# Gate and up of the last FFN as 2x2 blocks with seven products instead of eight

## What is computed

```python
D_FF_2 = ((8 * D_MODEL // 3 + 255) // 256) * 256      # 2816
h2 = rmsnorm_2(x, norm2_g[l])
g = jnp.einsum('bsd,df->bsf', h2, w_gate[l])
u = jnp.einsum('bsd,df->bsf', h2, w_up[l])
x = x + jnp.einsum('bsf,fd->bsd', jax.nn.silu(g) * u, w_down[l])
return rmsnorm_2(x, normf_g)
```

## Time and profile before

| | |
|---|---|
| time, median of 3 runs | 1824.26 us (1824.08 to 1824.57) |
| profiled execution: its span from first to last instruction | 1822.8 us |
| difference of the median to that span | 1.5 us |
| TensorE busy, mean granted clock | 1810.1 us (99%), 0.998 |
| VectorE, ScalarE, GpSimd busy | 938.6, 727.8, 272.3 us |
| last FFN, first gate matmul to last down matmul | 1451.3 to 1810.3 us |

### The profile page before, as it was taken

One profiled execution on the slowest core, in us unless ns is written; L12 is line 12 of the kernel. 1 busy time (PEld: TensorE's weight loads), 2 busy tenths in 40 slices (PEclk: granted clock), 3 DMA queues, 4 the chain that ended last, 5 costly groups with the idle time before them and its releaser, 6 DMA issues.

```text
span 1822.8 us, 21331 instructions
## 1 busy us (share of the span) xinstructions
PE 1810.1 (99%) x8733; PEld 1472.7 (81%) x8733; DVE 938.6 (51%) x1429; ACT 727.8 (40%) x1155; POOL 272.3 (15%) x241
## 2 busy tenths in 40 slices
PE   9999999999999999999999999999999999999998
PEld 7877788888888887878888888877777888888886
DVE  6878556443453456545653345458667443333324
ACT  5644444331332435654432233332567432212223
POOL 2001222210121200002221022103001222101210
PEclk9999999999999999999999999999999999999999
DMA  6121123222222333212223222232121132222221
GB/s 243 67 88 66 70 95 114 93 93 94 91 95 96 118 128 108 82 47 93 93 95 113 93 93 95 91 110 99 70 103 59 70 109 100 93 92 93 102 89 64
DMA packets 32337, 173.41 MB, mean 95 GB/s; under 512 B 4064, under 2 KB 6240, under 8 KB 14320
## 3 DMA queue, kind: packets, MB, share of 16 engines
q1 hardware_dynamic: 26848, 162.55, 25.0%
q10 hardware_dynamic: 5392, 9.51, 1.6%
HBM read 169.38 MB, written 2.13 MB: 94 GB/s over the span
## 4 chain that ended last, share of the span: by engine, by line
PE 96%; ACT 1%; DVE 1%; DMA 0%; POOL 0%; issue 0%; SPq 0%; ACTq 0%; DVEq 0%; POOLq 0%
PE ps L995 54%; PE ps L1299 20%; PE ps L929 7%; PE ps L1014 5%; PE ps L1141 2%; PE ps L1186 2%; PE ps L1166 2%; PE ps L1034 1%; PE ps L1225 1%; PE ps L1206 1%; DMA raw<-in_wall 0%; ACT PC L1543 0%; DVE WL L1806 0%; ACT WH L1375 0%; POOL sq L2326 0%
## 5 line engine op out<-in xcount | busy, mean ns | idle before, releaser
L995 PE MATMUL ps<-hH,WH 128*128 128x512 f32 x1456 | 570.9, 392 | 0.1
L1806 DVE TENSOR_TENSOR WL<-raw,WH 128x1024 fp32r<-128x1024 f32 (+2 forms) x308 | 377.3, 1264 | 368.1 <-ACT WH L1375 367.9
L995 PE MATMUL ps<-hH,WL 128*128 128x512 f32 x1456 | 566.7, 389 | 0.0
L995 PE MATMUL ps<-hL,WH 128*128 128x512 f32 x1456 | 566.7, 389 | 0.0
L1375 ACT ACTIVATE WH<-raw 128x1024 fp32r<-128x1024 f32 (+2 forms) x308 | 301.4, 1026 | 311.8 <-PE ps L1299 228.6
L995 PEld LDWEIGHTS ps<-hH,WH 128*128 128x128 f32 x1456 | 273.3, 188 | 65.3 <-issue 7.3
L995 PEld LDWEIGHTS ps<-hH,WL 128*128 128x128 f32 x1456 | 273.3, 188 | 57.0
L995 PEld LDWEIGHTS ps<-hL,WH 128*128 128x128 f32 x1456 | 273.3, 188 | 56.9 <-issue 1.0
L1299 PE MATMUL ps<-fL,WH 128*128 128x512 f32 x531 | 205.9, 388 | 0.0
L1299 PE MATMUL ps<-fH,WL 128*128 128x512 f32 x531 | 205.9, 388 | 0.0
L1299 PE MATMUL ps<-fH,WH 128*128 128x512 f32 x531 | 205.9, 388 | 0.0
(11 more groups left out here) (369 smaller groups left out, 2020.7 us busy)
## 6 DMA issues: line engine op xcount, KB each, us to landing
raw<-in_wall SPq DMA_DIRECT2D x140, 1024.0 KB, 4.6
raw<-in_wall SPq DMA_DIRECT2D x12, 768.0 KB, 4.0
bias<-in_bias ACTq DMA_DIRECT2D x12, 256.0 KB, 3.3
X<-in_xt SPq DMA_DIRECT2D x8, 256.0 KB, 8.9
CB<-rows ACTq DMA_DIRECT2D x8, 256.0 KB, 3.3
raw<-in_wall SPq DMA_DIRECT2D x4, 256.0 KB, 5.8
mrA<-in_memt ACTq DMA_DIRECT2D x4, 256.0 KB, 6.3
Mb<-m_rows ACTq DMA_DIRECT2D x4, 256.0 KB, 4.8
```

The lines of the kernel that those rows point to most:

```text
L995: mm = e.matmul(ps[b][:, 0:N], ww[:, k, c:c + 128], x[:, k, 0:N], start=(k == 0 and i == 0), stop=(k == 7 and i == 2))
L1806: e.tensor_tensor(WL[n % NCV][:, c], raw[n % NRAW][:, c], WH[n % NCV][:, c].bitcast(F32), ALU.subtract).then_inc(*mark("wl", n, x))
```

## The change

Only the last FFN changes (`WINO = (2,)`). Its first pair of units (block s = 0) is computed as before, in four tiles of 512 columns (steps `wg0`, `wu0`). For each of the ten later pairs, s = 1 to 10, the gate and up weights are cut in a 2x2 of blocks (even and odd k-tiles; gate and up) and the tokens in two halves of 256, and seven products (Strassen's, in Winograd's form) take the place of eight. Each product (`wp`) has K = 512 and 256 gate or up features: 4 k-tiles x 2 tiles x 3 parts = 24 matmuls of 256 columns. They run in the order q1, q5, q6, q3, q7, q2, q4. q1, q6, q7 and q4 add up in one PSUM bank; so q6 waits until ScalarE has copied the bank after q1 (`wcopy`), q7 until it has copied it after q6, q4 after q7. q5 and q3 share a second bank, q2 has a third.

Products 5, 6, 3 and 7 take sums of weight blocks, made on VectorE (`wsum`, 1024 columns each) ahead of their conversion; products 5, 6, 4 and 7 take sums of activation halves. Those are made by `wt`, once for each pair p = 0 to 3 of X tiles: a scaled copy of 256 columns on ScalarE, four scalar_tensor_tensor of 256 columns on VectorE (T5, T7, T6, T4), a rounding of 768 columns on ScalarE (TH), a subtraction of 768 columns on VectorE (TL). `wt` 0 and 1 stand behind the `res_norm` of tiles 5 and 6, `wt` 2 and 3 behind the two gate tiles of block 0. `wt7` overwrites part of hH and hL once block 0 is through.

Weights are converted in chunks of 1024 columns (`cconv`), four places of WH/WL in turn, so the conversion for product n+3 stands ahead of product n in the list and waits for product n-1. A block has seven chunks to convert where it had four. There are three raw buffers; per block two gate/up units and one down unit are loaded. `down` moves into the stream: after the products of a block come one or two pieces `wd` (24 matmuls of 512 columns each, one piece for s = 1 and 2, two from s = 3), and VectorE adds each output tile to X (`wx`; with the tail 48 additions where there were 16); the last 4 k-tiles stay as a tail. The number of down matmuls does not change. Per block VectorE also adds c12 and c11 from PSUM, multiplies by R (1024 columns), makes c22, z1 and z0; ScalarE copies four banks and does SiLU and H in 1024 columns, GpSimd y and L in 1024 columns each.

The core of the diff:

```diff
+WINO = (2,)
+PRODUCTS = (1, 5, 6, 3, 7, 2, 4)
...
+def wino_sequence():
+
+    out = []
+    for s in range(1, NSU):
+        out += [("q", s, q) for q in PRODUCTS] + [("d",) + x for x in down_pieces(s)]
+    return out
+
+
...
+            two(("U1", s), block(gate, g, 0), block(up, u, 0))
+            if x[2] != 1:
+                two(("U2", s), block(up, u, 1), block(gate, g, 1))
...
+                at = block_of(q)
+                if at:
+                    c["unit"], c["at"] = ROLE[i, at[0], s], at[1] * CHUNK
+                else:
+                    c["sum"] = {5: ((units[0], CHUNK), (units[1], 0)), 6: ((i, "q", s, 5), (units[0], 0)),
+                                3: ((i, "q", s, 6), (units[1], CHUNK)), 7: ((units[0], 0), (units[0], CHUNK))}[q]
+                    c["place"] = {5: 0, 6: 1, 3: 0, 7: 1}[q]
...
+                if nrm in WINO_OF and m in (5, 6):
+                    put("wt", WINO_OF[nrm], m - 5)
...
+    def ffn_wino(i, end):
+        late = []
+
+        def used(key):
+            done.add(("chunk", CHUNK_AT[key]))
+
+        for p, _ in enumerate(g_fm(1, FFN_NORMS[i], f"g{i}", "wg0")):
+            put("wt", i, 2 + p)
+        for _ in g_fm(1, FFN_NORMS[i], f"u{i}", "wu0"):
+            conv_ahead(len(UNITS))
+        flush_norms()
+        put("wt7", i)
+        for x in SEQUENCE:
+            conv_ahead(len(UNITS))
+            if x[0] == "d":
+                _, g, c = x
+                put("wd", i, g, c)
+                while late:
+                    put(*late.pop(0))
+                used((i, "d", g, c))
+                put("wx", i, g, c)
+                continue
+            _, s, q = x
+            put("wp", i, s, q)
+            while late:
+                put(*late.pop(0))
+            used((i, "q", s, q))
+            if q in (1, 5, 6, 7):
+                put("wcopy", i, s, q)
+            elif q == 3:
+                put("wc12", i, s)
+            elif q == 2:
+                put("wc11", i, s)
+                put("wgate", i, s)
+            else:
+                put("wz1", i, s)
+                late.append(("wz0", i, s))
+        while late:
+            put(*late.pop(0))
+        hread = ("wq", i, NSU - 1, 4)
+        if i == 2:
+            put("sqrt_table")
+        for mg in (0, 1):
+            n = ROLE[i, "T", mg]
+            now["unit"] = n + 1
+            conv_ahead(n + 2)
+            for gi, ks in TAIL[mg]:
+                for mi in range(4):
+                    put("wtail", i, mg, gi, mi, n, ks)
+                    if gi == 2:
+                        put("res_ffn", i, 1, 4 * mg + mi, hread)
+            done.add(n)
+        if end:
+            rstd(end, 60)
+
     def ffn(i, acts, end):
+        if i in WINO:
+            ffn_wino(i, end)
...
+                elif what == "wp":
+
+                    i, st, pn = a
+                    c = CHUNK_AT[i, "q", st, pn]
+                    kind = {1: "wA", 6: "wA", 7: "wA", 4: "wA", 5: "wD", 3: "wD", 2: "wB"}[pn]
+                    opens = pn in (1, 5, 2)
+                    if opens:
+                        b, before = bank((kind, i, st), {"wA": ("wg", "z", 0), "wD": ("wg", "c12"), "wB": ("wg", "c11")}[kind] + (i, st),
+                                         hold=kind == "wA")
+                        if before:
+                            w.wait_ge(*at(*before))
+                    b = BANK[kind, i, st]
+                    if not opens:
+                        w.wait_ge(*at("wcopy", i, st, {6: 1, 7: 6, 4: 7, 3: 5}[pn]))
+                    w.wait_ge(*at("wl", "c", c))
+                    W = [x.rearrange("p (k c) -> p k c", k=4) for x in chunk_slot(c)]
+                    for p in range(4):
+                        w.wait_ge(*at(*moving_at(i, pn, p)))
+                        H, L = moving(pn, p)
+                        for u in (0, 1):
+                            for n, (ww, x) in enumerate(((W[0], H), (W[0], L), (W[1], H))):
+                                mm = e.matmul(ps[b][:, 256 * u:256 * u + 256], ww[:, p, 128 * u:128 * u + 128], x,
+                                              start=(opens and p == 0 and u == 0 and n == 0),
+                                              stop=(p == 3 and u == 1 and n == 2), skip_group_check=True)
+                    mm.then_inc(*mark("wq", i, st, pn))
+                    FREED["chunk", c] = ("wq", i, st, pn)
...
+                elif what == "cconv":
+                    c = a[0]
+                    if CHUNKS[c]["sum"]:
+                        w.wait_ge(*at("wg", "sum", c))
+                    else:
+                        w.wait_ge(*loaded(CHUNKS[c]["unit"]))
+                    for b in W_BEFORE["chunk", c]:
+                        w.wait_ge(*at(*FREED[b]))
+                    e.activation(chunk_slot(c)[0], chunk_src(c), ACT.Copy).then_inc(*mark("wh", "c", c))
...
+                elif what == "wt":
+                    i, p = a
+                    st = FFN_NORMS[i]
+                    if p:
+                        w.wait_ge(*at("wg", "t", "L", i, p - 1))
+                    w.wait_ge(*at("xo", OUT_OF[i], 2 * p))
+                    e.activation(Tf[:, 3, :], X[:, 2 * p, 256:512], ACT.Copy, scale=col(st, 2 * p)).then_inc(
+                        *mark("wcopy", "t", "B", i, p))
+                    w.wait_ge(*at("wg", "t", 4, i, p))
+                    e.activation(TH[:, p, :, :], Tf[:, 0:3, :], ACT.Copy).then_inc(*mark("wcopy", "t", "H", i, p))
+
...
+                elif what == "wcopy":
+                    i, st, pn = a
+                    dst = {1: held_q1, 5: held_q5, 6: held_v, 7: held_w}[pn]
+                    w.wait_ge(*at("wq", i, st, pn))
+                    if st == 1:
+                        w.wait_ge(*(at("wg", "t", "L7", i) if pn in (6, 7) else at("wg", "t", "L", i, 3)))
+                    else:
+                        w.wait_ge(*at(*{1: ("wg", "c11"), 5: ("wg", "z", "c22"), 6: ("wg", "c12"), 7: ("wg", "z", 1)}[pn], i, st - 1))
+                    e.activation(dst[:, :, :], by_tile(BANK["wD" if pn == 5 else "wA", i, st]), ACT.Copy).then_inc(
+                        *mark("wcopy", i, st, pn))
+
...
+                    w.wait_ge(*at("wg", "ng", i))
+                    w.wait_ge(*at("wcopy", "t", "B", i, p))
+                    e.scalar_tensor_tensor(out=Tf[:, 0, :], in0=a0, scalar=g[:, 2 * p:2 * p + 1], in1=Tf[:, 3, :],
+                                           op0=ALU.mult, op1=ALU.subtract).then_inc(*mark("wg", "t", 5, i, p))
+                    w.wait_ge(*at("xo", OUT_OF[i], 2 * p + 1))
+                    e.scalar_tensor_tensor(out=T7f[:, p, :], in0=a3, scalar=g[:, 2 * p + 1:2 * p + 2],
+                                           in1=Tf[:, 3, :], op0=ALU.mult, op1=ALU.subtract).then_inc(
+                        *mark("wg", "t", 7, i, p))
+                    w.wait_ge(*at("wg", "t", 5, i, p))
+                    e.scalar_tensor_tensor(out=Tf[:, 1, :], in0=a3, scalar=ng[:, 2 * p + 1:2 * p + 2],
+                                           in1=Tf[:, 0, :], op0=ALU.mult, op1=ALU.subtract).then_inc(
+                        *mark("wg", "t", 6, i, p))
+                    w.wait_ge(*at("wg", "t", 6, i, p))
+                    e.scalar_tensor_tensor(out=Tf[:, 2, :], in0=a1, scalar=ng[:, 2 * p + 1:2 * p + 2],
+                                           in1=Tf[:, 1, :], op0=ALU.mult, op1=ALU.subtract).then_inc(
+                        *mark("wg", "t", 4, i, p))
+                    w.wait_ge(*at("wcopy", "t", "H", i, p))
+                    e.tensor_tensor(TL[:, p, :, :], Tf[:, 0:3, :], TH[:, p, :, :].bitcast(F32),
+                                    ALU.subtract).then_inc(*mark("wg", "t", "L", i, p))
+
+                elif what == "wt7":
+                    i = a[0]
+                    w.wait_ge(*at("wcopy", "t", "H7", i))
+                    e.tensor_tensor(hL[:, 0:8:2, 256:512], T7f[:, :, :], hH[:, 0:8:2, 256:512].bitcast(F32),
...
+                        w.wait_ge(*at("wsilu", i, st - 1))
+                    e.tensor_tensor(gs[:, :, 256:512], by_tile(BANK["wD", i, st]), held_v[:, :, :], ALU.add).then_inc(
+                        *mark("wg", "c12", i, st))
...
+                    R = Rsb[:, :].rearrange("p (o t) -> p o t", o=1).broadcast_to([128, 2, 512])
+                    e.tensor_tensor(gs[:, :, :], gs[:, :, :], R, ALU.mult).then_inc(*mark("wg", "r", i, st))
...
+                elif what == "wz1":
+                    i, st = a
+                    w.wait_ge(*at("wcopy", i, st, 7))
+                    w.wait_ge(*at("wcopy", i, st, 5))
+                    e.tensor_tensor(held_w[:, :, :], held_w[:, :, :], held_q5[:, :, :], ALU.add).then_inc(
+                        *mark("wg", "z", "c22", i, st))
+                    w.wait_ge(*at("wg", "z", "c22", i, st))
+                    w.wait_ge(*at("wpool", "y", i, st))
+                    e.scalar_tensor_tensor(out=yz[:, :, 256:512], in0=held_w[:, :, :], scalar=-1.0,
```

(106 more changed lines are left out.)

381 lines of the change are left out of this document (350 added, 31 removed).

## The result

| | before | after |
|---|---|---|
| median of the timed runs | 1824.58 us (1824.08 to 1825.29) | 1827.95 us (1827.56 to 1828.40) |
| profiled execution, span | 1822.8 us | 1826.6 us |
| mean granted clock | 0.998 | 0.995 |

The ratio is 1.0019, 95% interval 1.0011 to 1.0026: the change costs 3.4 us. The forecast was 1827.4.

The account below looks back on a forecast made before the run. TensorE, busy 99% of the span, was taken to bound the kernel. Median 1824.3 us less 16.0 of gain plus 19.1 of waits (7.0 + 2.8 + 2.6 + 3.4 + 3.3) gave 1827.4 us, 8-in-10 range 1818 to 1833.

Parts of the forecast that it names:

- TensorE's gain: Last FFN, blocks 1 to 10: 217.6 us of matmuls become 201.6 at 120.0 ns per 256-column matmul, gain 16.0 us.
- A conflict: VectorE's two-input SBUF operations stand while GpSimd works; without this the walk has 10.6 us of waiting, not 19.1.
- the walk: Going through the three queues of the last FFN in list order with prices, noting TensorE's waits: 19.1 us in sum.
- Step 1: Seam between output projection and FFN: activation sums delay WL by 1.4 us and hL7 by 5.6, first tile 7.0 late.
- Step 2: Blocks 0 and 1: VectorE's queue and GpSimd's L make TensorE wait 2.8 us for q5 and 2.6 for q6.
- Step 3: Blocks 2 and 3: late sum 3 holds WH of q3 and the bank copy after q1; waits 3.4 and 3.3 us.
- Steps 4 and 5: From block 3 on cost zero, with 3.8 us of cover per block; the end keeps its work and distances.
- The clock: First gate tile: the wait at hL7 brings matmuls at 1.2 GHz, 2.4 us more, 1829.8 us; chance 0.22.
- The other rivals: VectorE not held by GpSimd, 1818.9 us (0.18); activation sums free, 1816.5 (0.10); VectorE the bound in every block, 1835.4 (0.15).
- The signs: Wrong if hL7 lands before 1458, 256-column matmuls cost other than 120 ns, waits pass block 3, or the clock dips.

Follow-up runs that it names:

- experiment 4: Changed kernel with GpSimd's multiplications by R and low parts in the last FFN cut to 8 columns: 1820.43 us, ratio 0.9981 to the kernel before.
- experiment 2: Changed kernel with the four groups of activation sums moved behind the last X tile: 1826.17 us, ratio 1.0009 to the kernel before.
- experiment 1: Changed kernel with the first gate tile's matmuls of X tiles 0 to 6 issued twice: 1826.17 us, ratio 1.0008 to the kernel before.
- experiment 10: Kernel with two plain pairs, activation-sum groups 0 and 1 both behind gate tile 0, 2 and 3 behind up tiles 0 and 1: 1817.18 us, ratio 0.9960.
- experiment 5: Changed kernel with ScalarE's bank copy after q1 put ahead of WH of q3 from block 2 on: 1827.78 us, ratio 1.0016 to the kernel before.
- experiment 6: Changed kernel with VectorE's sums of weights cut to 8 columns from block 2 on: 1823.08 us, ratio 0.9990 to the kernel before.

## Why the prediction held, point by point

- **TensorE's gain, 16.0 us**: right. 168 matmuls take 20.15 us, 120 ns each, so the 256-column row with other operands carried over to the number. The kernel with three plain pairs gets 12.4 of 12.8 us by the same rate.
- **A conflict**: right as a mechanism. The low part beside GpSimd took 2.56 us and 1.22 without it (experiment 4). Its size in waits was put too high: without the conflict the walk had 8.5 us less of waits, and cutting GpSimd's operations took away 5.1 (of 7.5 us of time, the rest clock for the most part). The Trainium skill names this contention (GPSIMD Engine Reference, Specifications), and the trace agrees, 2.56 us against 1.22.
- **Step 1, the seam, 7.0 us**: 1.3 + 5.2 = 6.5, hL7 0.4 us earlier than walked. But "order of the queue" would have been the wrong lesson to draw: experiment 2 removes these waits and gets them back at q1, by the amount of work.
- **Step 2, block 1, 2.8 and 2.6 us**: 2.4 and 2.4.
- **Step 3, blocks 2 and 3, 3.4 and 3.3 us**: the place and the path were right, the size was not: 1.7 and 2.1 us. This term is the mis-sized one, by 2.9 us. Of that the shorter operations of GpSimd explain a little (2.38 and 2.41 us for 1024 columns in these blocks, not 2.58), and VectorE stood 2.5 and 2.9 us for the two landings, not 3.1. The slow q6 also gave VectorE 1.5 us to catch up; with that product at full clock (experiment 1) the two blocks wait 4.5 us by the distances of starts and not 3.8. So 0.7 of the 2.9 is the slow q6. What the rest is was not settled.
- **Steps 4 and 5, nothing**: right. From 1553 on the chain is TensorE's alone until down ends.
- **The clock** was a rival and not in the sum, and that was wrong. It came true beside the forecast: 2.2 us in the first gate tile, as the 2.4 taken there, and 1.6 in q6 of block 1, which I did not foresee. With it the waits and the clock make 18.9 us where the walk had 19.1 of waits: two errors, 3.8 us of clock missing and 4.0 of waits too much (2.9 of them in step 3), that cancel by luck. The total, 0.6 us from the measured one, is thus nearer than its terms. The other rivals' conditions did not come about: VectorE was held, the sums found no free time, and no wait goes on behind block 3.
- **The signs.** Of the four that I had named for a wrong prediction one came, the dip of the clock. And the chain is TensorE for 89% and not for over 95%: my own walk has VectorE lead from 1446 to block 3, some 100 us or 6% of the span, which I did not take off the 96% of before. VectorE is busy for 83% of 1550 to 1700, near the 85% named.

## What to carry to other kernels

Fewer products on TensorE are only worth something where the engine that makes their operands has the time; count that work over the stretch in which it is first needed, start-up sums and the reciprocal included, and let the plain form run until the backlog is gone. Here three plain pairs turned a loss of 3.4 us into a gain of 12.4, while reordering the same work only moved the waits (experiments 2 and 10). Count work put on GpSimd on VectorE's bill too, and count for each long wait of TensorE the slow matmuls behind it, unless another wait follows that would have eaten them.

## What the runs showed of the hardware

- The granted clock fell to 0.50 behind waits of TensorE. From start to start of two matmuls, gaps of 5.5 us (changed kernel), 6.4 us (sums later) and 3.9 us (sums early) each came with a low stretch. With shorter ones it varied. The gap of 2.6 us ahead of q5 came with one in experiments 1, 5 and 6, and not in the changed kernel, where it came with the next gap, of 2.5 us. The gap of 2.5 us with two plain pairs came without one, and with one once the copy was moved, at the same time of the execution (1505.2 and 1505.1). So the length of the gap alone does not decide, and by their mean clocks executions of one kernel can differ by such a stretch (experiment 4). What decides stays open. The Trainium skill (TensorE: Matmul & The Clock Gate, Why this matters for your kernels) warns of idle gaps; the rows agree, and show the fall behind short gaps too, though not each time.
- GpSimd is slowed by VectorE as well. Its ten low parts of this line took 3.07 us in the mean, where the one of block 0, at 1489.72, took 2.38; the group in the changed kernel (busy us, mean ns):

```profile
L3042 POOL TENSOR_TENSOR FL<-yz,FH 128x1024 fp32r<-128x1024 f32 x10 | 30.7, 3069 | 63.5 <-ACT FH L1852 63.5
```

The ten are of two kinds: three take 2.37 to 2.40 us and seven 3.36 or 3.37. Each of the seven starts 0.12 us after a sum of weights on VectorE has begun, and the three do not. One of the seven, with VectorE beside it:

```profile
1574.02 1.22 DVE L2300 TENSOR_TENSOR Wsum<-Wsum,raw 128x1024 f32<-128x1024 f32 x1
1574.14 3.37 POOL L3042 TENSOR_TENSOR FL<-yz,FH 128x1024 fp32r<-128x1024 f32 x1 [6.51 <-ACT FH L1852]
1575.15 3.43 DVE L2306 TENSOR_TENSOR WL<-Wsum,WH 128x1024 fp32r<-128x1024 f32 x1
```

In these rows the two engines take turns by whole instructions: the sum keeps its 1.22 us, GpSimd ends 2.3 us after it, and VectorE's low part ends 1.1 us after GpSimd, about its own time in each case. The one that starts first is not slowed.
